# Rotary positions and q, k norms of attention computed in the projection's last six weight tiles instead of in the table stage

## The reference

```python
def _attention_branch(q, k, v, z, q_norm_w, k_norm_w, row, col):
    q = q.reshape(Bsz, T, ATT_HEADS, ATT_HEAD_DIM)
    k = k.reshape(Bsz, T, ATT_KV_HEADS, ATT_HEAD_DIM)
    q = _axial_rope(_rmsnorm(q, q_norm_w), row, col)
    k = _axial_rope(_rmsnorm(k, k_norm_w), row, col)
    o = _block_attention(q, k, v)
    return (o.astype(jnp.float32) * jax.nn.silu(z.astype(jnp.float32))).astype(z.dtype)

def _rope(x, pos):              # d = 32; _axial_rope applies it to each half of a head
    rot = jnp.concatenate([-x32[..., d // 2:], x32[..., :d // 2]], axis=-1)
    return (x32 * cos + rot * sin).astype(x.dtype)
```

## Time and profile before

| | us |
|---|---|
| median of three runs | 4617.97 |
| the profiled execution's own time | 4623.46 |
| its span, first to last instruction | 4621.6 |
| projection tile 20 begins (layer 1) | 602.8 |
| table stage, layer 1 | 744.97 to 854.10 |
| table stage, layer 2 | 2992.18 to 3105.88 |
| mean granted TensorE clock over the span (share of full) | 0.933 |

### The profile page before, as it was taken

The page is one execution under the profiler, slowest core; times in us unless marked ns, Lnnn a source line. Parts: engine busy times, 40 slices in busy tenths (PEclk is TensorE's granted clock), DMA queues, the critical chain, the costliest instruction groups (busy, mean ns, idle before and its releaser), DMA issues. The chain is left out here.

```text
span 4621.6 us, 57733 instructions
## 1 busy us (share of the span) xinstructions
PE 4030.5 (87%) x19861; PEld 3100.3 (67%) x19861; DVE 2625.3 (57%) x3180; ACT 1865.6 (40%) x2592; POOL 716.0 (15%) x764
## 2 busy tenths in 40 slices
PE   3999997569979999987879999856997999999693
PEld 2788884369946666656758888725995666666473
DVE  5543003457768888874255400045676888888532
ACT  3221111235447777761132211112453777777310
POOL 0011101378500000000000110035862000000000
PEclk9999998789979999998989999968997999999896
DMA  6111113744520000016231111265455000000635
GB/s 238 62 69 68 55 68 133 174 116 137 148 66 24 23 23 23 23 45 207 105 127 69 55 68 68 83 174 136 122 158 118 23 23 23 23 23 16 169 143 193
DMA packets 327392, 418.00 MB, mean 90 GB/s; under 512 B 112496, under 2 KB 262372, under 8 KB 300076
## 3 DMA queue, kind: packets, MB, share of 16 engines
q1 hardware_dynamic: 322880, 386.57, 27.1%
q10 hardware_dynamic: 4352, 29.36, 2.4%
HBM read 267.95 MB, written 147.91 MB: 90 GB/s over the span
## 5 line engine op out<-in xcount | busy, mean ns | idle before, releaser
L1660 DVE TENSOR_REDUCE att_sb_part<-att_banks 128x1 f32<-128x512 f32 x1024 | 679.6, 685 | 165.7 <-PE att_banks L1561 157.1
L1648 ACT ACTIVATE att_sb_probs<-att_banks 128x1024 f32<-128x1024 f32 x512 | 525.0, 1025 | 445.9 <-PE att_banks L1579 445.7
L1678 DVE TENSOR_TENSOR att_sb_p_lo<-att_sb_probs,att_sb_p_hi 128x1024 fp32r<-128x1024 f32 x512 | 623.5, 1218 | 20.1 <-ACT att_sb_p_hi L1652 18.0
L1652 ACT ACTIVATE att_sb_p_hi<-att_sb_probs 128x1024 fp32r<-128x1024 f32 x512 | 543.3, 1061 | 16.2
L254 PE MATMUL proj_banks<-proj_sb_h_hi,proj_sb_w_hi 128*128 128x512 f32 x1600 | 518.9, 405 | 6.2 <-DVE proj_sb_w_lo L376 6.2
L254 PE MATMUL proj_banks<-proj_sb_h_lo,proj_sb_w_hi 128*128 128x512 f32 x1600 | 516.0, 404 | 0.0
L254 PE MATMUL proj_banks<-proj_sb_h_hi,proj_sb_w_lo 128*128 128x512 f32 x1600 | 515.9, 404 | 0.0
L1561 PE MATMUL att_banks<-att_sb_k,att_sb_q 128*128 128x512 f32 x1024 | 402.5, 424 | 44.2 <-DMA att_sb_q<-att_q 34.7
L376 DVE TENSOR_TENSOR proj_sb_w_lo<-proj_sb_w_raw,proj_sb_w_hi 128x1024 fp32r<-128x1024 f32 x52 | 69.2, 1330 | 640.5 <-ACT proj_sb_w_hi L312 640.5
L1578 PE MATMUL att_banks<-att_sb_q,att_sb_k 128*128 128x512 f32 x1024 | 411.9, 402 | 15.5 <-DVE att_sb_v_lo L1717 15.5
L996 PE MATMUL dn_banks<-dn_sb_room 128*128 128x128 f32 x3072 | 379.1, 283 | 50.5 <-DMA dn_sb_room<-proj 22.5
(11 more groups left out here) (221 smaller groups left out, 5690.5 us busy)
## 6 DMA issues: line engine op xcount, KB each, us to landing
proj<-proj_sb_out SPq DMA_DIRECT2D x52, 1024.0 KB, 4.4
dn_sb_kq<-proj SPq DMA_DIRECT2D x64, 512.0 KB, 5.2
proj_sb_w_raw<-in_w_in SPq DMA_DIRECT2D x52, 516.0 KB, 5.2
dn_sb_room<-proj SPq DMA_DIRECT2D x32, 768.0 KB, 5.1
att_sb_q<-att_q SPq DMA_DIRECT2D x64, 256.0 KB, 2.9
out_sb_x<-x_res SPq DMA_DIRECT2D x16, 1024.0 KB, 6.7
x_res<-out_sb_x SPq DMA_DIRECT2D x16, 1024.0 KB, 4.2
out_sb_w_raw<-in_w_out SPq DMA_DIRECT2D x24, 512.0 KB, 4.9
```

Of the source, the lines that this page charges most:

```text
L1648: nc.scalar.activation(probs[:, pair % 2], ps[:, 2 * (pair % 2):2 * (pair % 2) + 2, :], ACT.Exp, scale=SCALE).then_inc(s["exp_done"], 1)
L1652: nc.scalar.activation(p_hi[:, pair % SLOTS], probs[:, pair % 2], ACT.Copy).then_inc(s["hi_done"], 1)
L1660: nc.vector.tensor_reduce(part[:, w // NQ, w % NQ:w % NQ + 1], ps[:, 4 + w % 2, :], AX.X, ALU.max) \
L1678: nc.vector.tensor_tensor(p_lo[:, pair % SLOTS], probs[:, pair % 2], p_hi[:, pair % SLOTS].bitcast(F32), ALU.subtract).then_inc(s["lo_done ...
```

## The change

The weight columns of q and k are reordered on the host so that a pair of tiles holds, for four heads, the 32 "first" dims of each (tile 2m) and the 32 "second" dims (tile 2m + 1): heads 0 to 3, heads 4 to 7, and a third pair with the two k heads in 64 of its 128 partitions and v in the others. The rotation then needs no swap between partitions. Its work is cut into 12 units (three pairs, four quarters of 512 tokens), two units in each of the gate tiles 20 to 25 of the projection. A unit: load both tiles' quarter back from `proj` (`ab`), load the inverse rms of its heads from `qk_rows`, spread over 32 partitions each by the DMA (`inv`); four DVE products, a POOL addition, a DVE scaling, the high part on ACT, the low part on DVE, and four stores into `att_q` or `att_k`, two of the high and two of the low part. The sums of squares are now by quarter of the partitions (four columns), finish one tile earlier, and get root, reciprocal and transposes in tiles 18 and 19. The table stage keeps the DeltaNet tables and v, which it now loads as two transfers of 64 partitions.

```diff
@@ input_projection, SP @@
+                def load_unit(n):
...
+                    if n % PAIR_TILES == 0:
+                        if n:
+                            sp.wait_ge(s["products"], n)
+                        sp.dma_start(rope, a.rope[:, :, cols].rearrange("f p t -> p f t")).then_inc(s["rope_loaded"], 16)
+                    if n >= 2:
+                        sp.wait_ge(s[f"rope_stored{u}"], 64 * (n // 2))
+                    sp.dma_start(ab[u][0:parts], a.proj[T_AQ + 2 * pair:T_AQ + 2 * pair + 2, 0:parts, cols]
+                                 .rearrange("f p t -> p f t")).then_inc(s[f"ab_loaded{u}"], 16)
+                    heads = parts // QUARTER
+                    sp.dma_start(inv[u][0:parts], a.qk_rows[4 * pair:4 * pair + heads, cols].unsqueeze(1)
+                                 .broadcast_to([heads, QUARTER, QB])).then_inc(s[f"inv_loaded{u}"], 16)
+
+                def store_unit(n):
...
+                    for src, low in ((ab[u], 0), (yy[u], DH)):
+                        sp.wait_ge(s["lo" if low else "hi"], n + 1)
+                        for half in range(2):
+                            row = low + half * QUARTER
+                            sp.dma_start(dst[:, row:row + QUARTER, at:at + QB], src[0:parts, half, :]) \
+                                .then_inc(s[f"rope_stored{u}"], 16)
...
+                for t in range(ROPE_TILE, N_TILES):
+                    n = 2 * (t - ROPE_TILE)
+                    load_weights(t)
+                    if n:
+                        store_unit(n - 1)
+                    load_unit(n + 1)
+                    store_unit(n)
+                    load_unit(n + 2)
+                    store_tile(t)
+                store_unit(ROPE_UNITS - 1)
@@ input_projection, PE @@
+                tile_half(i, 0, 0, [[lambda n=n: square_sum(i - 1, 0, n)] for n in range(NC)])
...
+                tile_half(i, 1, 0)
+                pe.wait_ge(s["inv_rms"], 1)
+                nc.tensor.transpose(ps[:, 6, 0:P], rms_flat[:, 0:P], c.ident[:])
+                nc.tensor.transpose(ps[0:N_ROWS * NC - P, 7, 0:P], rms_flat[:, P:N_ROWS * NC], c.ident[:]) \
+                    .then_inc(s["turned"], 1)
+                tile_half(i, 1, 1)
@@ input_projection, POOL @@
+                for n in range(ROPE_UNITS):
+                    parts, u = rope_unit(n)[2], n % 2
+                    pool.wait_ge(s["products"], n + 1)
+                    nc.gpsimd.tensor_tensor(xx[u][0:parts], xx[u][0:parts], yy[u][0:parts], ALU.add).then_inc(s["added"], 1)
@@ input_projection, ACT @@
                     for half in range(2):
+                        if extra:
+                            high_part(extra[half])
                         e = evacuate(t, u, half, out[:, u, half * HALF:(half + 1) * HALF], func)
...
+                for t in range(ROPE_TILE, N_TILES):
+                    plain(t // 2, t % 2, ACT.Silu, t + 1 < N_TILES, extra=[2 * (t - ROPE_TILE), 2 * (t - ROPE_TILE) + 1])
@@ input_projection, DVE @@
+                for t in range(ROPE_TILE, N_TILES):
+                    if t + 1 < N_TILES:
+                        split_w(t + 1, (t + 1) % 2)
+                    for n in (2 * (t - ROPE_TILE), 2 * (t - ROPE_TILE) + 1):
+                        rope_products(n)
+                        rope_scale(n)
+                        rope_low(n)
@@ token_inputs @@
-                sp.dma_start(v[:], a.proj[T_AV]).then_inc(s["v_loaded"], 16)
-                sp.dma_start(swap[:], a.swap).then_inc(s["const_loaded"], 16)
...
-                for t in range(N_QK):
-                    sp.dma_start(q[:, t, :], a.proj[T_AQ + t]).then_inc(s[f"x_loaded{t}"], 16)
+                for kv in range(KV_HEADS):
+                    sp.dma_start(v[kv * DH:(kv + 1) * DH], a.proj[T_AK + kv, DH:P]).then_inc(s["v_loaded"], 16)
...
-                swap_quarters(0)
-                for t in range(N_QK):
...
-                products(0)
-                for t in range(N_QK):
```

More of the change, by code:

```diff
@@ L47, with rope_unit @@
 WCOLS = KT * P + 8
+STATS = T_Z - T_Q
+QUARTER = P // 4
+PAIR_TILES = 3
+N_ROWS = ATT_HEADS + KV_HEADS
+ROPE_UNITS = PAIR_TILES * NQ
+ROPE_TILE = T_Z + 2
+def rope_unit(n):
+    pair, quarter = n % PAIR_TILES, n // PAIR_TILES
+    return pair, quarter * QB, P if pair < PAIR_TILES - 1 else P // 2
 W_BA = 2 * ITEMS
@@ L250, in tile_half @@
                             if between:
-                                between.pop(0)()
+                                for extra in between.pop(0):
+                                    extra()
                             for n in range(2):
@@ L474, in token_inputs @@
         rk2 = b.sbuf("rk2", [P, DN_HEADS, NC])
[L475 to L486, removed]
+        rows = b.sbuf("rows", [P, P])
         v = b.sbuf("v", [P, SEQ])
@@ L593, in _ @@
                 nc.scalar.activation(c.v_scale[:], kk[:].rearrange("p h c -> p c h"), ACT.Sqrt).then_inc(s["act_step"], 1)
[L594 to L603, removed]
-                        for src, at in ((hi, 0), (lo, DH)):
-                            act.dma_start(dst[head, at:at + DH], src[part, t % 2, :].bitcast(F32)) \
-                                .then_inc(s[f"stored{t % 2}"], 16)
-                for t in range(N_QK):
-                    act.wait_ge(s["scaled"], t + 1)
-                    if t >= 2:
-                        act.wait_ge(s[f"stored{t % 2}"], 64 * (t // 2))
-                    nc.scalar.copy(hi[:, t % 2, :], q[:, t, :]).then_inc(s["hi"], 1)
-                    if t:
-                        store(t - 1)
-                store(N_QK - 1)
-                act.wait_ge(s["stored0"], 3 * 64)
-                act.wait_ge(s["stored1"], 2 * 64)
             @block.vector
@@ L1958 @@
     pass
+FIRST_DIMS = [*range(0, DH // 4), *range(DH // 2, 3 * DH // 4)]
+SECOND_DIMS = [d + DH // 4 for d in FIRST_DIMS]
 def constants():
@@ L2042 @@
 _SHAPES = ["x_in", "w_in", "w_ba", "norm_w", "decay", "dn_norm_w", "qk_norm_w", "w_out",
-           "masks", "ident", "ones", "halves", "rope", "quarter", "swap", "halves_t"]
+           "masks", "ident", "ones", "quarters", "rope", "quarter"]
 def lay_out(x, norm_w, w_in, conv_w, a_log, dt_bias, dn_norm_w, q_norm_w, k_norm_w, w_out, final_norm_w):
@@ L2069, in lay_out @@
     g["dn_norm_w"] = np.asarray(dn_norm_w)[:, :, None]
[L2070 to L2072 removed]
+    norm_cols = []
+    for v in (np.asarray(q_norm_w), np.asarray(k_norm_w)):
+        first, second = np.tile(v[:, FIRST_DIMS], (1, 4)), np.tile(v[:, SECOND_DIMS], (1, 4))
+        norm_cols += [first, second]
+    g["qk_norm_w"] = np.stack(norm_cols, axis=2)
     g["w_out"] = np.asarray(w_out).reshape(depth, KT, P, KT, P).transpose(0, 3, 2, 1, 4).reshape(depth, KT, P, KT * P)
```

252 lines of the change are left out of this document (139 added, 113 removed).

## The result

The changed kernel takes 4637.05 us (median of 5 runs, 4629.95 to 4643.62) against 4617.97: the ratio is 1.0035, with a 95% interval of 1.0024 to 1.0045. It is slower, by some 16 us by the ratio and 19 by the medians; the prediction had 4606 and "faster" as the slightly likelier side (0.43 against 0.41).

The account below looks back on a forecast made before the run. Now PE bounds the projection, chains and DMA the table stage; after the change DMA bounds the projection. Table stages -166.2 us and projection +153.8 give -12.4: median 4618.0 becomes 4606, own range 4580 to 4635.

Parts of the forecast that it names:

- Table stage: In both layers, with q and k work moved out, it falls to 28.3 us each, saving 166.2 us together.
- Confinement: In the units' transfers, outermost dimension 4 means four DMA engines at 102 GB/s: stores 10.3 us, `inv` 2.57 a unit.
- Rival 4: In the projection, no transfer is confined and PE stays the limit: 4457 us; chance 0.05.
- `ab` 1.25 (512 KB on 16 engines): In each unit's 16.0 us period, the load of both tiles' quarter takes 1.25 us on all engines.
- the 418 GB/s taken for the tile's store and weights: In the projection's DMA sum, the full-share rate of a 128-partition store; five tiles' stores 12.5 us, three weight loads 3.9.
- Nine periods: In the gate tiles, the load and store chain up to unit 9, at 16.0 us a unit: 144.0 us.
- Rival 1: In the units' stores, each burst starts slow, 88 GB/s over 1 MB, 14.9 us a unit: 4651 us; chance 0.28.
- Rival 2: In the units' transfers, four engines stay at half speed, 53 GB/s, 24.7 us a unit: 4874 us; chance 0.06.
- the end: After 187.1 us of the stretch: unit 11's load, the last stores and semaphore clearing, up to 218.5 us.
- Unit compute hidden: In the gate tiles, a unit's compute is 8.4 us; two units and the split, 18.0, fit under 22.5 a tile.
- Clock: Rival 5: TensorE's clock falls in the projection's new gaps, 45 us a tile at 1.2 GHz: 4675 us; chance 0.03.
- my own case: The forecast for the whole kernel, 4606 us with range 4580 to 4635; chance 0.45.

Follow-up runs that it names:

- the first experiment: The changed kernel with each unit's stores issued as one transfer per head and part (outermost 32) instead of across heads: 4458.2 us, ratio 0.9649 to the kernel before.

## Why the prediction was wrong

The forecast was 12.4 us faster and the profiled run came out 13.6 slower, so some 26 us over both layers decide it. Step by step:

- **Table stage: right.** 28.3 forecast, 27.2 and 27.1 measured; v's matmuls at an offset of 9.8 (10.3), the store of `b_rows` at 20.5 (20.9).
- **Confinement: right, `inv` too.** Share and rate are the ones taken from the earlier trace rows, 98 to 106 GB/s on four engines and about 50 on two, and halving or doubling the confined transfer of the stores moved the kernel as its weight in the sum says (83 for 87 us, 161 for 165); taking `inv` out of it gave 14.7 us where 29 to 44 were due. The rule of the Trainium skill that the prediction cited ("DMA: Bandwidth & Descriptors", section "Why a DMA increments its semaphore by 16 and not by 1") agrees with the shares of these runs, with those of the four groups of 8 rows if they count as merged; for `inv` by the 104 GB/s at a share of 0.27. Rival 4, PE as the limit when nothing is confined, had 4457; the first experiment measured 4458.
- **The failed step: "`ab` 1.25 (512 KB on 16 engines)", a term of the period that was too small, and with it the 418 GB/s taken for the tile's store and weights.** Each period's loads start from engines that have gone quiet. In the period from 647.74 the 512 KB run from 648.75 to 651.1, 2.4 us. The rest of that period is as forecast or shorter: 13.2 us of four- and two-engine transfer (12.87), and 1.4 from issue to first byte and from last byte to landing (1.9). It lasts 17.0 in place of 16.0. In the period from 664.73, with the tile's store and weights, 2.1 MB take 7.0 us where the sum had 5.0, 297 GB/s from 665.5 to 672.5:

```profile
665.00:666.00 1.00, 1.00 (x6) 0.81 (x5) 0.00 (x0) 0.00 (x0) 0.00 (x0) 1.00 0.34 31
666.00:667.00 1.00, 1.00 (x6) 0.80 (x5) 0.00 (x0) 0.00 (x0) 0.00 (x0) 1.00 0.83 188
667.00:668.00 1.00, 1.00 (x6) 0.79 (x5) 0.00 (x0) 0.00 (x0) 0.00 (x0) 1.00 1.10 428
...
670.00:671.00 1.00, 1.00 (x5) 0.77 (x5) 1.00 (x2) 0.00 (x0) 0.00 (x0) 1.00 0.88 220
671.00:672.00 1.00, 1.00 (x6) 0.81 (x5) 0.24 (x1) 0.00 (x0) 0.68 (x1) 1.00 1.01 338
```

The start is slow, but so is a later part (220 and 338), whose cause no run shows. This period lasts 21.2 in place of 19.8. In the period from 685.97, which begins with a k unit's smaller load, the load and `inv` are through at about 688.7, and the stores behind them have only 57 to 74 GB/s until 692 (windows of 0.5 us). It lasts 18.0 where the sum, with the load of cosines and sines, had 17.3. Nine periods come to 172.4 instead of 164.2 us; how the 8.2 are split over these three places was not worked out.
- **Rival 1 was half right.** Unit 0's stores start at 25 to 63 GB/s, and 14.0 us pass from issue to landing (12.2 forecast). It does not happen to each burst: behind a q unit's load and `inv` the stores run at 98 GB/s and more (674 to 685) and the slow microseconds fall on the load; behind a k unit's load the stores are slow again (689 to 692). Its 4651 was too high and my 4606 too low: one charged a slow start to every burst of stores, the other to nothing. Its second argument, that 2 KB rows cost more than 4 KB rows, does not show on four engines: both run at 98 to 106 GB/s.
- **Rival 2 fell.** Past the first microseconds four engines that read blocks 32 partitions apart run at 98 to 106 GB/s, not at 53.
- **The size of it.** Unit 0 comes 2.2 us late, the nine periods 8.2, the end 1.7 (33.1 for 31.4): 12.1 in layer 1. Both layers are 24.7 over the forecast, the tables 2.3 under, the rest of the kernel 3.5 over, together the 26 from 4611 to the profiled 4637. The 3.5 are less than what the rest differs by from one profiled run to another (4100 to 4124 us). The other 5 us is that before's profiled run stood 5.5 above its median and this one doesn't. With three buffers, and the stores as they were, 26 and 30 us a layer go, and the kernel is 0.96% faster than before.
- **Unit compute hidden: right**, at slightly other sizes: the four products take 2.7 us (2.6), the addition holds DVE for 2.5 and not 1.9, and from the first product to the end of the low part unit 0 takes 8.9 and not 8.4. (Two of the expectations above say 9.3 and 8 us for this work or for its part up to the high part; the rows give 8.9 and 7.6.) With stores per head there was still room for it.
- **Clock: right that it hides.** The granted clock is 0.83 over the stretch in place of 0.99, and PE is busy 149.7 us where it had been 134.9; but PE is idle for 80.9 us of the stretch, in waits that end with ACT. Without the gaps (first experiment) the clock is back at 0.98.
- **The chance.** Break-even lay at 13.42 us of transfer a unit for a forecast of 12.87. The nine periods came out 0.9 us longer each than forecast, more than that margin, so the 0.45 for my own case was too sure. A slow start stood in the earlier trace rows already, at 53 GB/s, where I had given it to a rival alone.

## What to carry to other kernels

Read the outermost dimension of every transfer: moving work under a busy engine pays only if its transfers use all DMA engines; here the same bytes per head instead of across heads were worth 179 us. In a chain of load, compute and store that runs through two buffers, price the first microseconds of each transfer after a quiet moment from windows of 1 us, not from the steady rate, and multiply by the number of periods. A third buffer hides much of it even where the transfers stay slow.

## What the runs showed of the hardware

- Some transfers start slowly on quiet engines: stores on four engines show 25, 39, 63, then 100 GB/s, with and without DVE at work; loads on all engines, from their first bytes at 665.6, 31, 188, then 428. Not all do. A tile's store in the kernel before starts from rest and has 393 GB/s in its first microsecond (the window at 739.50 in the earlier trace rows); the one before it is

```profile
738.50:739.50 1.00, 0.00 (x0) 0.00 (x0) 0.00 (x0) 0.25 (x1) 0.00 (x0) 1.00 0.00 0
```

So quiet engines alone are not the cause; stores were slow from 689 to 692 with no rest just before them, too. Whether it is the direction, the rows, or engines that read partitions 32 apart (theory F) stays open, as the test that was meant for the last changed the number of engines instead.
- An issue of a 64 KB store holds SP for 0.43 us or so; behind a slow burst it holds it for much longer. In the three-buffer run two issues took 7.08 us together.
- Transfers confined to two engines do not spread over others when several are queued: with pairs of heads the share stayed at 0.13 to 0.14.
- Writing the DRAM side as four neighbouring groups of rows did not confine the stores (share 0.53 to 0.59).
- With the share at 0.92 to 0.98, stores of 128 KB in 2 KB rows ran at 207 to 266 GB/s, against 393 at 0.94 for a tile's store of 1 MB.
